# A hybrid diffusion trunk on one core: the mixer's 32 weight chunks per round move from the doubling levels to the round's beginning, middle and tail

## The reference

```python
mod = silu(c) @ w_ada[l] + b_ada[l]           # 2048 x 12288 weights, one vector per group
sh_a, sc_a, g_a, sh_f, sc_f, g_f = split(mod, 6)
proj = (rmsnorm(x) * (1 + sc_a) + sh_a) @ w_in[l]
o = concat(attention, short_conv, rwkv_mixer) @ w_out[l]
x = x + g_a * rmsnorm(o)
x = x + g_f * rmsnorm(swiglu(rmsnorm(x) * (1 + sc_f) + sh_f))
```

```python
sa = S @ (-kk_t)
S = S * w_t + outer(sa, kk_t * a_t) + outer(v_t, k_t)
y_t = S @ r_t
```

## Time and profile before

| what | value |
|---|---|
| three runs | 3161.4, 3172.85, 3172.89 us (median 3172.85) |
| profiled execution | 3162.76 us, span 3161.0 us |
| TensorE busy | 90% of the span |
| VectorE, ScalarE, GpSimd busy | 52%, 35%, 5% |
| mean granted TensorE clock | 0.94 |
| HBM traffic | 599.62 MB, 190 GB/s over the span |
| rounds of layer 0, stage matmuls start | 364.4, 447.1, 528.4, 610.6 us |

### The profile page before, as it was taken

How to read it: one execution, slowest core, us unless ns; L and a number is a source line. 1 busy time by engine, 2 the same in 40 slices (tenths; PEclk the granted TensorE clock), 3 DMA queues, 4 the chain that set the end, 5 groups by cost and what they waited for, 6 DMA issues and landing times.

```text
span 3161.0 us, 48889 instructions
## 1 busy us (share of the span) xinstructions
PE 2838.3 (90%) x17315; PEld 2170.7 (69%) x17315; DVE 1647.9 (52%) x2172; ACT 1094.4 (35%) x1377; POOL 165.9 (5%) x209
## 2 busy tenths in 40 slices
PE   6899777789899999999878997777898999999997
PEld 1578545567688888888616885555676888888885
DVE  0465544444655555555505655455356555555554
ACT  0244322224344444444203443222234444444442
POOL 1000111110000000000010001111000000000000
PEclk9899888899899999999998998888998999999998
DMA  9765455565365555555496554555644555555552
GB/s 365 242 182 157 133 208 208 205 219 181 115 191 186 187 190 187 188 190 186 133 336 208 167 164 150 189 205 203 221 166 133 186 188 190 186 190 188 186 189 90
DMA packets 317183, 599.62 MB, mean 190 GB/s; under 512 B 23184, under 2 KB 29288, under 8 KB 316584
## 3 DMA queue, kind: packets, MB, share of 16 engines
q1 hardware_dynamic: 309488, 592.90, 56.9%
q10 hardware_dynamic: 7608, 5.60, 0.6%
HBM read 595.28 MB, written 3.15 MB: 189 GB/s over the span
## 4 chain that ended last, share of the span: by engine, by line
PE 75%; issue 9%; DVE 7%; DMA 5%; ACT 2%; POOL 1%; DVEq 1%; ACTq 0%; SPq 0%; POOLq 0%
PE bank L758 73%; DMA rawW<-in_w_ada 5%; PE bank L1104 1%; DVE xs L1285 1%; DVE sigaa L1548 0%; DVE ksq L1461 0%; DVEq L286 0%; ACT L563 0%; SPq L335 0%; DVE BF L1487 0%; DVE tf L1266 0%; DVE AE L1487 0%; POOL qst L667 0%; DVE cs L1445 0%; DVE x L1287 0%
## 5 line engine op out<-in xcount | busy, mean ns | idle before, releaser
L1213 DVE TENSOR_TENSOR loW<-rawW,hiW 128x1024 fp32r<-128x1024 f32 x592 | 725.0, 1226 | 739.3 <-ACT hiW L376 739.1
L376 ACT ACTIVATE hiW<-rawW 128x1024 fp32r<-128x1024 f32 x592 | 627.1, 1061 | 964.7 <-PE bank L758 962.9
L758 PE MATMUL bank<-hiW,actH 128*128 128x512 f32 (+1 forms) x2304 | 901.9, 391 | 19.5 <-DVE loW L1213 17.3
L758 PE MATMUL bank<-loW,actH 128*128 128x512 f32 (+1 forms) x2304 | 894.7, 388 | 0.0
L758 PE MATMUL bank<-hiW,actL 128*128 128x512 f32 (+1 forms) x2304 | 894.2, 388 | 0.0
L758 PEld LDWEIGHTS bank<-hiW,actH 128*128 128x128 f32 x2304 | 436.3, 189 | 111.2 <-DVE loW L1213 18.1
L758 PEld LDWEIGHTS bank<-hiW,actL 128*128 128x128 f32 x2304 | 436.0, 189 | 89.3
L758 PEld LDWEIGHTS bank<-loW,actH 128*128 128x128 f32 x2304 | 436.3, 189 | 87.7 <-issue 1.0
L758 PE MATMUL bank<-rawW,csR 128*32 128x512 f32 x1536 | 271.6, 663 | 54.5 <-DMA rawW<-in_w_ada 40.8
L758 PE MATMUL bank<-hiW,ffH 128*128 128x512 f32 x704 | 281.8, 400 | 3.2 <-DVE ffL L1579 3.2
L758 PE MATMUL bank<-loW,ffH 128*128 128x512 f32 x704 | 280.9, 399 | 0.0
(11 more groups left out here) (243 smaller groups left out, 2261.2 us busy)
## 6 DMA issues: line engine op xcount, KB each, us to landing
rawW<-in_w_ada SPq DMA_DIRECT2D x384, 512.0 KB, 6.9
rawW<-in_w_gate SPq DMA_DIRECT2D x176, 512.0 KB, 3.5
rawW<-in_w_up SPq DMA_DIRECT2D x176, 512.0 KB, 3.5
rawW<-in_w_down SPq DMA_DIRECT2D x176, 512.0 KB, 3.6
rawW<-in_w_in SPq DMA_DIRECT2D x144, 512.0 KB, 3.5
rawW<-in_w_out SPq DMA_DIRECT2D x64, 512.0 KB, 3.6
rawW<-in_w_in SPq DMA_DIRECT2D x16, 160.0 KB, 2.3
x<-in_x_prompt SPq DMA_DIRECT2D x1, 1024.0 KB, 7.0
```

The costliest lines, as they stand in the source:

```text
L376: act.activation(hiW[:, c % LEAD, :, 0:width], rawW[:, c % SLOTS, :, 0:width], ACT.Copy).then_inc(hi_ready, 1)
L758: return pe.matmul(out, a, b, start=start, stop=stop, skip_group_check=True)
L1213: TT(loW[:, slot, :, 0:width], rawW[:, slot, :, 0:width], hiW[:, c % LEAD, :, 0:width].bitcast(F32), ALU.subtract).then_inc(lo_ready, 1)
```

## The change

All 32 chunks of a round keep their order and their products. They are issued elsewhere: tile qa whole at the very beginning of the round, ahead of the wait for rw_stage; six chunks of qa + 2 behind VS (after a wait for the row copy that frees bank 7) and two behind A/B; tile qa + 4 in the levels, one chunk in each of the first four half-levels and two in each of the last two; tile qa + 6 in four pairs in the tail, into bank 3: behind S1, W2, SA and ST. rows3 has two halves. The turns of rows move with the tiles: two stay in the levels, one stays between S1 and W2, one comes after the variance. VectorE's row copies move to behind ksq, behind the bonus, behind the levels and behind the subtraction of the mean. The loop over v is written out on TensorE and VectorE, and stays a loop on ScalarE.

```diff
-                rows3 = sb("rows3", [P, NW], F32, ph2)
+                rows3 = sb("rows3", [P, 2, NW], F32, ph2)
...
+                    ada_chunks(qa, 0, 8, 7)
                     pe.wait_ge(rw_stage, it + 1)
...
+                    pe.wait_ge(rr_v, it * 4 + 1)
+                    ada_chunks(qa + 2, 0, 6, 7)
                     pe.wait_ge(rw_sig, it + 1)
-                    ada_chunks(qa, 0, 4, 7)
...
                         e.then_inc(rw_A, 1)
-                    ada_chunks(qa, 4, 6, 7)
+                    ada_chunks(qa + 2, 6, 8, 7)
...
                     mm(bank[3][:, 0:256], blk1, flat(nrm[:])).then_inc(rw_bon, 1)
-                    ada_chunks(qa, 6, 8, 7)
...
-                            if w == 0:
+                            if w == 0 and v < 2:
                                 pe.wait_ge(rr_v, it * 4 + v + 1)
-                                turn_rows(rows3[:], 5).then_inc(rp_T, 1)
+                                turn_rows(rows3[:, v], 5).then_inc(rp_T, 1)
                             if w == 0 and first:
                                 pe.wait_ge(rw_bg, it + 1)
+                                pe.wait_ge(rr_v, it * 4 + 2)
...
-                            ada_chunks(q, 4 * w, 4 * w + 4, 4)
-                    levels(it * (2 * LEVELS), it * (2 * LEVELS - 2), qa + 2, 0, first=True)
-                    with pe.Fori(1, LEVELS // 2) as v:
-                        levels(pe.snap(it * (2 * LEVELS) + v * 4), pe.snap(it * (2 * LEVELS - 2) + v * 4),
-                               pe.snap(qa + 2 + v * 2), v)
+                            c0 = (0, 1, 2, 3, 4, 6, 8)[2 * v + w]
+                            ada_chunks(qa + 4, c0, (0, 1, 2, 3, 4, 6, 8)[2 * v + w + 1], 4)
+                    for v in range(LEVELS // 2):
+                        levels(it * (2 * LEVELS) + v * 4, it * (2 * LEVELS - 2) + v * 4, v, first=v == 0)
...
                         e.then_inc(done, 1)
+                        ada_chunks(qa + 6, 4 * half, 4 * half + 2, 3)
                         if half == 0:
-                            pe.wait_ge(rr_v, it * 4 + 4)
-                            turn_rows(rows3[:], 5).then_inc(rp_T, 1)
+                            pe.wait_ge(rr_v, it * 4 + 3)
+                            turn_rows(rows3[:, 0], 5).then_inc(rp_T, 1)
...
                             e.then_inc(rw_W2, 1)
+                            ada_chunks(qa + 6, 2, 4, 3)
...
                     e.then_inc(rw_ST, 1)
+                    ada_chunks(qa + 6, 6, 8, 3)
...
                     mm(bank[2][:, 256:512], blkm, yy[1]).then_inc(rw_var, 1)
+                    pe.wait_ge(rr_v, it * 4 + 4)
+                    turn_rows(rows3[:, 1], 5).then_inc(rp_T, 1)
```

On VectorE:

```diff
                     TT(ksq[:], kk[:], kk[:], ALU.mult).then_inc(rw_sq, 1)
+                    tile_done(qa)
+                    dve.tensor_copy(rows3[:, 0], bank[7][:]).then_inc(rr_v, 1)
...
-                    tile_done(qa)
-                    dve.tensor_copy(rows3[:], bank[7][:]).then_inc(rr_v, 1)
+                    tile_done(qa + 2)
+                    dve.tensor_copy(rows3[:, 1], bank[7][:]).then_inc(rr_v, 1)
...
-                        tile_done(q)
-                        dve.tensor_copy(rows3[:], bank[4][:]).then_inc(rr_v, 1)
...
+                    tile_done(qa + 4)
+                    dve.tensor_copy(rows3[:, 0], bank[4][:]).then_inc(rr_v, 1)
...
                     TT(y0, y0, bank[2][:, 0:256], ALU.subtract).then_inc(rw_yc, 1)
+                    tile_done(qa + 6)
+                    dve.tensor_copy(rows3[:, 1], bank[3][:]).then_inc(rr_v, 1)
...
+                    dve.wait_ge(rp_T, it * 4 + 4)
+                    dve.tensor_copy(mod[:, bass.ds(f * 32 + 88, 8)], bank[5][:, 0:8])
```

More of the change, by code:

```diff
@@ L1001, in rwkv, with levels @@
                     mm(bank[3][:, 0:256], blk1, flat(nrm[:])).then_inc(rw_bon, 1)
-                    ada_chunks(qa, 6, 8, 7)
                     pe.wait_ge(rw_bv, it + 1)
                     settle(pe)
-                    def levels(n, m, q, v, first=False):
+                    def levels(n, m, v, first=False):
                         for w in range(2):
@@ L1534, in rwkv @@
                     e.then_inc(rw_R2, 1)
-                    dve.wait_ge(rp_T, it * 4 + 4)
-                    dve.tensor_copy(mod[:, bass.ds(f * 32 + 88, 8)], bank[5][:, 0:8])
+                    dve.wait_ge(rp_T, it * 4 + 3)
+                    dve.tensor_copy(mod[:, bass.ds(f * 32 + 80, 8)], bank[5][:, 0:8])
                     y0, y1, y2, y3 = yy
```

## The result

The changed kernel takes 3152.8 us at the median of 8 runs (3146.6 to 3154.8), the kernel before 3169.0 at the median of 8 (3161.4 to 3172.9). The ratio is 0.9947, with a 95% interval of 0.9936 to 0.9958: 0.5% faster, 16 us instead of the 60 that were forecast. The profiled execution took 3154.8 us, 8 less than the one of before: the profile of before is a low run of its kernel, the one of after the highest of its own, so what the two traces explain is 8 us and not 16.

What follows compares the result with a forecast made beforehand. TensorE was taken as the bound, with weight work in the levels paid in full. The terms -70 + 5 + 0.4 - 4 + 8 + 1 = -59.6 us led to a forecast of 3109 us, range 3088 to 3143.

Steps and rivals of the forecast that it cites:

- the levels: Levels of each round: 24 chunks become 8 and a turn of rows leaves, 8.7 us a round, -70 us.
- the code: Written-out level loop: 7 instruction packets instead of 5, fetched only in each layer's first round, +1 us.
- the front: Stage matmuls of rounds 2 to 4 sometimes find the clock high: -4 us, bounds 0 and -7.
- the tail: S1 to mean: chunks mostly fill waits and the clock holds, +5 us; +14 up to +21 if it does not.
- rival 3: Levels do not shrink because the chain over ScalarE, VectorE and GpSimd sets a half-level: 3190 us, chance 0.03.
- The price of a chunk: Levels: each chunk moved out of a half-level gives back its 0.48 us on TensorE.
- a cold start: Start of levels at fallen clock: only chunks and turns double, under 2 us a round, kept for the range.
- Rival 1: Jump back to the next round: program does not stay, each round refetches and stalls, +27 us, 3136, chance 0.10.
- The estimate of eight packets: TensorE's program store: 128 KiB holds about eight packets, so the written-out round would still just fit.
- The beginning: Round start: turn and eight chunks fit the 7.39 us wait for gS in rounds 2 to 4; round 1 stages later, +8.
- the middle: Between VS and KR: six chunks fit TensorE's waits and their loads come in time, 0 us.
- Rival 2: Tail and round beginnings: clock does not hold and the eight chunks come late, 3140 us, chance 0.12.

Runs made afterwards that it cites:

- experiment 1: Kernel before with only the loop over level pairs written out on TensorE and VectorE: 3198.6 us against 3168.1, ratio 1.0106.
- experiment 3: Changed kernel with all level chunks and turns in the first pass, last two passes written out instead of looped: 3185.4 us against 3165.7 of the kernel before.
- experiment 4: Changed kernel with level loop kept, three chunks behind the last half-level, looped chunks on other data: 3139.9 us against 3165.0 before; changed kernel beside it 3154.7.

## Why the prediction was wrong

On the two profiled executions the forecast was -59.6 and the result -8. Of the difference, 46 us are the levels and 21 the code; the front (-11) and the tail (-4) came out better than forecast.

**The levels, -70 forecast, -24 measured: the step that failed.** The regime was read rightly: work in the levels is paid in full, the loop over ScalarE, VectorE and GpSimd closes in 3.4 us (3.2 forecast), and rival 3 was not so. Two prices were wrong. The price of a chunk was taken as a quarter of a group of four, 0.48 us. Its two products fill two of four strips, and the row shows 0.98 us for one chunk and for two; four single chunks a round lose 2.0 us, 16 in all. The sign of it stood in the earlier trace rows: a mean of 598 ns a record, against 1.85 / 16 = 0.12 us on the path, so the records overlap. And the trace of before has single chunks and pairs, which take the same time:

```profile
20.01 1.05 PE L758 MATMUL bank<-rawW,csR 128*32 128x512 f32 x4 [0.44 <-DMA rawW<-in_w_ada]
...
467.23 1.07 PE L758 MATMUL bank<-rawW,csR 128*32 128x512 f32 x8
```

And the clock: I wrote that small matmuls are paced by issue, so that a cold start costs under 2 us a round, kept that for the range, and put nothing for it into the sum. The cold U group took 1.97 us instead of 1.15, the turn 1.86 instead of 1.05, and the first half-level 3.5 us more than the 3.0 that my terms give it, of which 0.5 is the strips of its single chunk and 3.0 the clock. In six of eight rounds the second half-level began cold too (5.0 to 5.4 us instead of 4.27), 0.7 a round on average. 8 x 3.7 is 30 us. 16 and 30 make the missing 46, give or take 4 us of smaller terms.

**The code, +1 forecast, +22 measured.** Rival 1 came true, with a chance of 0.10: a stall of 4.25 to 4.85 us where 3.5 to 6 were named, at each of six crossings, 22 us against its 27. By itself this would have left the time at some 3131, inside the range; the levels alone put it outside. The failed step here was the inference that five packets which stay mean that seven stay. What the runs show is that 5 stay and 7 do not. The estimate of eight packets, worked out from the 128 KiB that the Trainium skill's "Runtime: NRT & Kernel Launch" (Instruction fetch mechanics) gives TensorE, did not hold either. Another rule of that section, a stall at a taken branch whose target lies outside what is kept, is what the 4.3 us look like; that only two pages are kept does not fit the loop of 5 packets that stays. Experiments 1 and 3 show the size: 30 and 52 us for the loop written out and nothing else. In the change's own layout it is smaller, since the levels there have no halt for instructions: experiment 4, freed of its three-chunk group, gives 23.

**The beginning.** Right in direction and too cautious: the stage matmuls found the clock high in all rounds and KR came 1.47 us earlier, so the front gave -15, not -4. The eight chunks delay round 1 by 4 us a layer, as forecast (+8). That this could be avoided by one wait behind them was not seen. Four of the six chunks in the middle did wait for their loads, 0.26 to 0.31 us each in round 2, hidden behind the 3.18 us that TensorE then still waited for VectorE's be.

**The tail.** Right in its mechanism: Y group to mean took 5.12 us in every round, 4.25 and the pair, and S1 to variance 12.8 to 13.0, where the terms give 13.0. That the sum was +0.6 and not +5 lies mostly in the kernel before: three of its rounds took 13.6 to 13.8 us here, not round 2's 12.8. Rival 2's falling clock did not happen there. (The 14 us that rival 3 names for the sum without the levels are 10; they leave out the -4 of the beginning.) The loads were in time: no wait for rawW stands ahead of the stage.

Not settled: why the clock falls ahead of the levels in some rounds and not in others, why the halts inside the levels are so unequal between layouts, and how much of the growth in experiments 1 and 3 is halts and how much the clock behind them. A case where the round's program lies between five and seven packets was not tried.

## What to carry to other kernels

Writing out an inner loop inside an outer one is a change of its own: look at the instruction queue's packets by window, and at issue idle inside groups, before and after, and time it alone. Price a moved piece of work from rows in which it stands alone, not by dividing a group whose members overlap. When work leaves a place, ask what the engine's clock does there without it: here two chunks of filler ahead of the levels were worth more than the microsecond they cost.

## What the runs showed of the hardware

- A written-out round whose first pass brought 7 instruction packets brought 8 or 9 in every later one (25 to 27 in three), with a halt of 3.9 to 5.0 us at the jump; a looped round with 5 packets brought 0 or 1 in three rounds.
- With instructions arriving during the round, TensorE also halted inside a group of matmuls, up to 3.72 us in a bare half-level (experiment 3) and 2.22 us in one with four chunks (experiment 1); the changed kernel itself had no such halt in its levels.
- Two products in different 32-column strips overlap: 4 records and 8 records of 128x512 both took 0.98 us to the next group, 12 and 16 records about 1.9.
- At 1.2 GHz (granted clock 0.50) even a U group, 32 records of 64x64 fp32 matmuls, slowed from 1.15 to 1.97 us, and the eight records of a turn of rows, 2 columns wide, from 1.05 to 1.86 us.
